# Two-block transformer forward pass on one core: the first block's attention loads the query latent's weights first, scores the second token half first, and turns keys after queries

## The reference, cut to what matters

```python
h = x @ w_in                                   # -> query latent c_q (256), k, v (2 heads x 64), k_idx (128), w_idx (8)
c_q = rms_norm(c_q, g_cq)
q, q_idx = c_q @ w_uq, c_q @ w_iq              # 16 heads x 64, 8 index heads x 128
k_idx = layer_norm(k_idx, g_ik, b_ik)
q, k, q_idx, k_idx = rope of each              # the first few columns of a head
# per block of 128 queries:
score = sum over index heads of w_idx * relu(q_idx . k_idx), causal
sel = the 64 keys of highest score             # per query
p = softmax of q . k over the selected keys; o = p . v
out = o @ w_o
```

## Time and profile before

| what | value |
|---|---|
| median of the three runs shown | 1112.74 us (1112.64 to 1114.21) |
| the profiled execution's own time | 1112.98 us |
| its span, first to last instruction | 1111.2 us |
| PE busy (matmuls) | 1081.2 us, 97% of the span |
| ACT busy | 547.6 us, 49% |
| DVE busy | 402.7 us, 36% |
| POOL busy | 775.8 us, 70% |
| chain of waits | PE 90%, DVE 7%, ACT 1%, DMA 1% |
| DMA | 186.45 MB, mean 168 GB/s |

### The profile page before, as it was taken

The page is one execution under the profiler, slowest core; times in us unless marked ns, Lnnn a source line. Parts: engine busy times, 40 slices in busy tenths (PEclk is TensorE's granted clock), DMA queues, the critical chain, the costliest instruction groups (busy, mean ns, idle before and its releaser), DMA issues.

```text
span 1111.2 us, 15697 instructions
## 1 busy us (share of the span) xinstructions
PE 1081.2 (97%) x6654; PEld 946.2 (85%) x6654; DVE 402.7 (36%) x741; ACT 547.6 (49%) x713; POOL 775.8 (70%) x201
## 2 busy tenths in 40 slices
PE   8978999999999997999999999999999999999997
PEld 7867888888889996888888899999999988888885
DVE  4674411119644787511110152821274233111103
ACT  6583453443357764544444256465565346343520
POOL 4723698788588741888878768686674768988880
PEclk9999999999999998999999999999999999999999
DMA  9211665555455431675555356454442555555541
GB/s 367 82 39 39 235 224 185 189 189 190 153 207 176 147 115 40 214 258 190 190 189 179 124 180 221 168 190 142 161 152 76 190 179 219 188 183 178 177 147 38
DMA packets 27445, 186.45 MB, mean 168 GB/s; under 512 B 3168, under 2 KB 3424, under 8 KB 5872
## 3 DMA queue, kind: packets, MB, share of 16 engines
q1 hardware_dynamic: 25184, 178.83, 46.4%
q10 hardware_dynamic: 2192, 6.62, 1.8%
HBM read 184.39 MB, written 1.05 MB: 167 GB/s over the span
## 4 chain that ended last, share of the span: by engine, by line
PE 90%; DVE 7%; ACT 1%; DMA 1%; issue 1%; DVEq 0%; SPq 0%; ACTq 0%
PE ps L380 27%; PE ps L382 27%; PE ps L381 27%; PE ps L1223 1%; DVE arena L2223 1%; PE ps L1370 1%; PE ps L2063 1%; PE ps L1088 1%; DMA stage<-in_tiles 1%; DVE arena L828 1%; DVE arena L850 1%; PE ps L2061 0%; PE ps L713 0%; DVE small L835 0%; DVE arena L1014 0%
## 5 line engine op out<-in xcount | busy, mean ns | idle before, releaser
L364 POOL TENSOR_TENSOR wl<-stage,wh 128x2048 fp32r<-128x2048 f32 x166 | 763.5, 4622 | 297.1 <-ACT wh L360 265.9
L360 ACT ACTIVATE wh<-stage 128x2048 fp32r<-128x2048 f32 (+1 forms) x168 | 319.9, 1906 | 114.4 <-DMA stage<-in_tiles 113.8
L380 PE MATMUL ps<-wh,xh 128*128 128x512 f32 (+2 forms) x832 | 306.1, 368 | 3.0 <-DVE xl L1642 1.6
L382 PE MATMUL ps<-wh,xl 128*128 128x512 f32 (+2 forms) x832 | 302.1, 363 | 0.0
L381 PE MATMUL ps<-wl,xh 128*128 128x512 f32 (+2 forms) x832 | 301.7, 363 | 0.0
L380 PEld LDWEIGHTS ps<-wh,xh 128*128 128x128 f32 x832 | 157.1, 189 | 27.3 <-DVE xl L1642 1.8
L382 PEld LDWEIGHTS ps<-wh,xl 128*128 128x128 f32 x832 | 157.0, 189 | 24.7
L381 PEld LDWEIGHTS ps<-wl,xh 128*128 128x128 f32 x832 | 157.2, 189 | 23.3
L380 PE MATMUL ps<-xh,wh 128*128 128x256 f32 x464 | 133.1, 287 | 0.0
L382 PE MATMUL ps<-xh,wl 128*128 128x256 f32 x464 | 131.3, 283 | 0.0
L381 PE MATMUL ps<-xl,wh 128*128 128x256 f32 x464 | 131.3, 283 | 0.0
(11 more groups left out here) (365 smaller groups left out, 1174.7 us busy)
## 6 DMA issues: line engine op xcount, KB each, us to landing
stage<-in_tiles SPq DMA_DIRECT2D x167, 1024.0 KB, 4.9
arena<-in_ln_g ACTq DMA_DIRECT2D x4, 512.0 KB, 3.6
arena<-in_ln_b ACTq DMA_DIRECT2D x4, 512.0 KB, 5.2
arena<-in_x_t SPq DMA_DIRECT2D x1, 1024.0 KB, 5.2
x_res<-in_x SPq DMA_DIRECT2D x1, 1024.0 KB, 20.4
out<-x_res SPq DMA_DIRECT2D x4, 256.0 KB, 2.1
stage<-in_tiles SPq DMA_DIRECT2D x1, 544.0 KB, 7.3
arena<-in_pre_mix_norm ACTq DMA_DIRECT2D x1, 512.0 KB, 7.7
```

Source lines behind the costliest of these rows:

```text
L360: nc.scalar.activation(wh[:, ring(n), part], stage[:, ring(n), part], ACT.Copy).then_inc(hi_done, 1)
L364: nc.gpsimd.tensor_tensor(wl[:, ring(n), :], stage[:, ring(n), :], wh[:, ring(n), :].bitcast(F32), ALU.subtract).then_inc(lo_done, 1)
L380: mm(out_, lh, rh, start=start, stop=False, skip_group_check=skip)
L382: return mm(out_, ll, rh, start=False, stop=stop, skip_group_check=skip)
```

## The change

Tile 0 is now the query latent's, loaded whole right behind `x_t`, and tile 1 the index keys' (1088 columns). ACT makes tile 0's high part in four quarters and only then issues the loads of positions and constants; DVE makes the low parts in quarters, and PE multiplies quarter by quarter. The latent has its own banks (0 and 3). Half 1's index queries, scores and selection come before half 0's; the index keys' rope stands behind the first index queries' rope on DVE; all of tile 3's products come late; the mask is made before the rope of half 1's queries. ACT's high parts have other places (tiles 8, 9 and 10 now stand together before the first exponentials), and warm-ups are moved. A line of "..." leaves out lines.

```diff
+    columns(w_att, 0, 256)
     tiles.append(np.concatenate([keys, np.zeros((P, TW - KD * IW), keys.dtype)], axis=1))
-    columns(w_att, 0, 256)
...
+            if n == 1:
+                sp.dma_start(stage[:, 1, 0:KD * IW], A["tiles"][1, :, 0:KD * IW]).then_inc(stage_in[1], 16)
...
-        his = [0]
+        his = [1]
...
-            first_low(dve, 0)
+            for c in range(4):
+                if c < 3:
+                    dve.wait_ge(first_hi.sem, c + 1)
+                else:
+                    dve.wait_ge(hi_done, 1)
+                first_low(0, slice(c * QUARTER, (c + 1) * QUARTER))
+            dve.wait_ge(hi_done, 2)
+            first_low(1, slice(0, KD * IW))
             dve.wait_ge(pos_in, 16)
             dve.wait_ge(c_in, 16)
...
-            first_low(dve, 1)
...
-            setup_loads(act)
             act.wait_ge(xt_in, 16)
             for c in range(4):
                 nc.scalar.activation(two(xh, c), two(x_raw, c), ACT.Copy).then_inc(xh_done.sem, xh_done.up())
+            act.wait_ge(stage_in[0], 16)
+            for c in range(4):
+                part = slice(c * QUARTER, (c + 1) * QUARTER)
+                ins = nc.scalar.activation(wh[:, 0, part], stage[:, 0, part], ACT.Copy)
+                if c < 3:
+                    ins.then_inc(first_hi.sem, first_hi.up())
+                else:
+                    ins.then_inc(hi_done, 1)
+            setup_loads(act)
...
-            keep_warm(7, 14)
+            keep_warm(7, 12)
+            for c in range(4):
+                pe.wait_ge(first_lo.sem, c + 1)
+                pe.wait_ge(x_ready.sem, x_ready.due(pe))
+                for m in range(2):
+                    for k in range(2 * c, 2 * c + 2):
+                        o = k * 256 + m * P
+                        last = mm3(ps[:, CQ_BANK[m], 0:T], (wh[:, 0, o:o + P], wl[:, 0, o:o + P]),
+                                   (xh[:, k, :], xl[:, k, :]), k == 0, k == KD - 1)
+            last.then_inc(used, 1)
...
-            tile_a(pe, 1, 0)
...
-            keep_warm(7, 6)
...
+            def keys_part(t, ks):
+                x = slice(t * P, (t + 1) * P)
+                for k in ks:
+                    o = k * 256
+                    last = mm3(ps[:, 2, t * T:(t + 1) * T], (xh[:, k, x], xl[:, k, x]),
+                               (wh[:, 3, o:o + T], wl[:, 3, o:o + T]), k == 0, k == KD - 1)
+                return last
+
+            def weigh(t, bank, width):
+                pe.wait_ge(dw_ready.sem, dw_ready.due(pe))
+                for h in range(IH):
+                    if h % (2 if t else 4) == 0:
+                        pe.wait_ge(relu_done.sem, relu_done.due(pe))
+                    last = mm(ps[:, bank, 0:width], dw[:, t * IH + h, :], relus[t][:, h, :], start=h == 0, stop=h == IH - 1)
+                last.then_inc(score_ps.sem, score_ps.up())
...
             pe.wait_ge(cq_ready.sem, cq_ready.due(pe))
-            query(2, 0, (4, 5)).then_inc(iq_ps.sem, iq_ps.up())
             pe.wait_ge(sq_done.sem, sq_done.due(pe))
             for t in range(2):
...
-            query(2, 1, (6, 7)).then_inc(used, 1)
-            index_turn(0)
+            query(2, 1, (6, 7)).then_inc(iq_ps.sem, iq_ps.up())
+            query(2, 0, (4, 5)).then_inc(used, 1)
+            index_turn(1)
+            pe.wait_ge(rs_cq.sem, 1)
...
+            late = (1, 3, 6, 7)
...
+            index_turn(0)
+            weigh(1, 0, T)
...
-            tile_b(pe, 3, [(1, 0, ps[:, 2, T:2 * T])])
+            low_ready(pe, 3)
+            keys_part(0, range(0, 4))
+            weigh(0, 1, P)
+            keys_part(0, range(4, KD))
+            keys_part(1, range(KD)).then_inc(used, 1)
+            pe.wait_ge(scored.sem, 2)
             query(4, 0, (1, 3)).then_inc(q_ps.sem, q_ps.up())
             query(4, 1, (6, 7)).then_inc(used, 1)
...
-            keep_warm(5, 4)
-            pe.wait_ge(q1_done.sem, q1_done.due(pe))
-            pe.wait_ge(scored.sem, 2)
-            for h in range(KD):
-                for t in range(2):
-                    last = nc.tensor.transpose(ps[:, 4 + h // 2, h % 2 * T + t * P:h % 2 * T + (t + 1) * P],
+            for t in range(2):
+                if t:
+                    pe.wait_ge(q1_done.sem, q1_done.due(pe))
...
-                if h % 2:
-                    last.then_inc(qt_ps.sem, qt_ps.up())
-            keep_warm(1, 8)
-            pe.wait_ge(kpad_done.sem, kpad_done.due(pe))
-            pe.wait_ge(qt_done.sem, qt_done.due(pe, 4))
-            pe.wait_ge(sel_done.sem, 1)
+                    if t and h % 2:
+                        last.then_inc(qt_ps.sem, qt_ps.up())
...
+                if i == 0:
+                    pe.wait_ge(kpad_done.sem, kpad_done.due(pe))
+                    pe.wait_ge(sel_done.sem, 1)
+                if i < 3:
+                    pe.wait_ge(qt_done.sem, (1, 2, 4)[i])
...
-            attend_pe(pe, HEADS // 2, logits, weighted)
+            attend_pe(pe, HEADS // 2, logits, weighted, 11)
...
+            act.wait_ge(used, 1)
+            act.wait_ge(c_in, 16)
+            for k in range(2):
+                last = nc.scalar.activation(hh[:, 20 + k, :], ps[:, CQ_BANK[k], 0:T], ACT.Copy, scale=gt[:, 44 + k:45 + k])
+            last.then_inc(cqh_done.sem, cqh_done.up())
...
+            hi_until(act, 3)
+            late_loads(act)
+            act.wait_ge(cq_ready.sem, cq_ready.due(act))
...
+            setup_act2(act)
...
-            hi_until(act, 3)
-            act.wait_ge(used, 2)
-            act.wait_ge(c_in, 16)
...
-            hi_until(act, 4)
...
+            hi_until(act, 4)
...
-            index_plain(0)
             index_plain(1)
+            index_turned(1)
+            for c, b in enumerate((1, 3, 6, 7)):
...
+                if c == 0:
+                    index_plain(0)
             index_turned(0)
             hi_until(act, 5)
-            index_turned(1)
-            hi_until(act, 6)
...
-            hi_until(act, 7)
+            hi_until(act, 6)
             act.wait_ge(used, 4)
...
-            hi_until(act, 8)
+            act.wait_ge(q_ps.sem, q_ps.due(act))
...
+            hi_until(act, 7)
+            act.wait_ge(kd_ps.sem, kd_ps.due(act))
...
-            act.wait_ge(kd_ps.sem, kd_ps.due(act))
...
             hi_until(act, 10)
...
+            dve.wait_ge(cqh_done.sem, cqh_done.due(dve))
+            for k in range(2):
...
+            last.then_inc(cq_ready.sem, cq_ready.up())
             ki = bank2(1)[:, :, 0:ID]
-            dve.wait_ge(used, 1)
+            dve.wait_ge(used, 2)
...
             dve.wait_ge(rs_cq.sem, rs_cq.due(dve))
+            index_rope(1)
+            keys_rope()
+            dve.wait_ge(kt_ps.sem, kt_ps.due(dve))
+            V.tensor_copy(kit, ps[:, 3, P:3 * P]).then_inc(kt_ready.sem, kt_ready.up())
+            dve.wait_ge(used, 3)
             index_rope(0)
...
+            V.tensor_copy(score[:, P:2 * P], ps[:, 0, 0:P])
+            V.tensor_tensor(score[:, 2 * P:3 * P], ps[:, 0, P:T], causal, ALU.min).then_inc(scored.sem, scored.up())
             dve.wait_ge(scored.sem, 1)
-            for i in range(4):
+            for i in range(5):
+                best_eight((1,))
+            dve.wait_ge(score_ps.sem, score_ps.due(dve))
+            V.tensor_tensor(score[:, 0:P], ps[:, 1, 0:P], causal, ALU.min).then_inc(scored.sem, scored.up())
+            dve.wait_ge(scored.sem, 2)
+            for i in range(TOPK // 8 - 5):
+                best_eight((1, 0))
+            for i in range(5):
                 best_eight((0,))
-            dve.wait_ge(score_ps.sem, score_ps.due(dve))
-            V.tensor_copy(score[:, P:2 * P], ps[:, 4, 0:P])
-            V.tensor_tensor(score[:, 2 * P:3 * P], ps[:, 4, P:T], causal, ALU.min).then_inc(scored.sem, scored.up())
-            dve.wait_ge(scored.sem, 2)
-            for i in range(TOPK // 8 - 4):
-                best_eight((0, 1))
-            for i in range(4):
-                best_eight((1,))
-            dve.wait_ge(used, 5)
...
             hi_until(act, 2)
-            late_loads(act)
-            setup_act2(act)
             dsa_act(act)
...
-            for n in range(2, 8):
+            for n in range(2, 7):
                 lo(pool, n)
             dsa_pool(pool)
+            lo(pool, 7)
```

More of the change, by code:

```diff
@@ L384, in low_ready @@
         def low_ready(pe, n):
-            if n < 2:
-                pe.wait_ge(first_lo.sem, n + 1)
+            if n == 1:
+                pe.wait_ge(first_lo.sem, 5)
             else:
@@ L694, in dsa_pe @@
             last.then_inc(kt_ps.sem, kt_ps.up())
-            tile_b(pe, 3, [(0, 0, ps[:, 2, 0:T])], done=False)
-            index_turn(1)
             pe.wait_ge(kt_ready.sem, kt_ready.due(pe))
+            late = (1, 3, 6, 7)
+            for h in range(IH):
+                if h % 4 == 0:
+                    pe.wait_ge(iqt_done.sem, iqt_done.due(pe))
+                last = mm(ps[:, late[h // 2], h % 2 * T:(h % 2 + 1) * T], iqt[:, h, P:T], kit, start=True, stop=True)
+                if h % 2:
```

(49 more changed lines are left out.)

88 lines of the change are left out of this document (36 added, 52 removed).

## The result

| | before | after |
|---|---|---|
| median of 12 runs | 1113.22 us | 1117.32 us |
| lowest and highest | 1112.64, 1120.80 | 1114.90, 1118.53 |
| profiled execution, its span | 1112.98, 1111.2 us | 1117.47, 1115.7 us |
| mean granted clock | 0.996 | 0.991 |
| first division | 68.57 | 72.53 |

The ratio is 1.0029 (95% interval 1.0020 to 1.0038), slower by more than the 0.2% that can be told from no change; the medians lie 4.10 us apart, and the new one is 1.5 us above the top of the range. Two executions of those behind this document, one of the kernel before at 1350.09 us and one of e5_forecast at 1201.0, ran at a mean granted clock of 0.75 and 0.85 and stand in no ratio. "First division" is DVE's RECIPROCAL of the first pair of heads, the point at which the forecast ended.

What follows compares the result with a forecast made beforehand. PE, busy 97% of the span, was taken as the bound, passing front changes on one for one. Logits 2.4 us earlier, then a third rounding, gave 67.1 - 66.6 = +0.45 us: 1113.2 us against the median, range 1110.8 to 1115.8.

Steps and rivals of the forecast that it cites:

- The term of 0.7 us for the landing after the last packet: Load of positions and constants: estimated 0.7 us from the last packet moved to the landing.
- the whole of 10.1 us: Load of positions and constants: 10.1 us from issue at 8.7 to landing at 18.8.
- Case (b): Late constants, issued not before the fourth quarter rounding: +1.4 us, 1114.6; chance 0.13.
- case (e): ACT's table switches cost twice 1.28 us, as if ACT had to run empty first: +2.6, 1115.8; chance 0.03.
- 1.4 us before DVE comes to them, so it hides: Index queries: PE is through at 27.5, ahead of DVE's rope at 28.9, so they add no time.
- case (c): PE's clock falls after idling before the index queries, matmuls near 0.6 us: +1.8, middle 1115.7; chance 0.13.
- ACT's three roundings: Tiles 8, 9, 10 before the first exponentials: 3 x 1.82 = 5.5 us, to 67.1, first division at 69.05.
- tile 7's is moved behind it: POOL before the loop: tile 6 ends near 50.4, 1.2 us before the keys' rope needs POOL; tile 7's work follows that rope.
- the 71 that the prediction had named as its limit: First division of the attention loop: the forecast is wrong if it comes before 67 or after 71.
- (d): The third rounding doesn't hold the exponentials, earlier logits passed on, no DVE wait before first division: -2.4, 1110.6; chance 0.09.
- from here the loop is as before: Attention loop from the first division on: no change, leaving the sum at +0.45 us.

Runs made afterwards that it cites:

- e5_forecast: Changed kernel with POOL's tile 8 low part behind the loop and ten warm-ups before PE's wait for the latent: 1114.01 us, ratio 0.9988.
- e4_rounds: Changed kernel with tiles 7 and 8 rounded in ACT's idle time behind tile 6, leaving two roundings before the exponentials: 1115.17 us, ratio 1.0017.
- e12_forecast_warm: e5_forecast with nine warm-ups behind the third logits in the loop: 1113.25 us, ratio 0.9994.
- e1_pool: Changed kernel with POOL's low part of tile 8 moved behind the loop's last division: 1115.25 us, ratio 1.0009.
- e8_port_before: Kernel before, with POOL starting tile 8's low part only when the first logits are in PSUM: 1116.69 us, ratio 1.0024.
- e3_consts: Changed kernel with positions and constants issued first in ACT's program, as before the change: 1111.98 us, ratio 0.9984.
- e7_behind: e6_all with tiles 9 and 10 also rounded behind the attention loop: 1108.00 us, ratio 0.9929.
- e11: Changed kernel with fifteen warm-ups behind the third logits: 1115.94 us, ratio 1.0015.
- e6_all: Changed kernel with the edits of e1_pool, e3_consts and e4_rounds together: 1108.17 us, ratio 0.9943.
- e10_control: Kernel before, with tiles 9 and 10 rounded behind the attention loop and POOL's tile 8 low part behind the divisions: 1113.79 us, ratio 0.9995.
- e2_warm: Changed kernel with ten warm-ups ahead of PE's wait for the latent's low part: 1115.58 us, ratio 1.0016.
- e9_loopwarm: Changed kernel with thirty warm-ups behind the third logits: 1117.87 us, ratio 1.0034.

## Why the prediction was wrong

**Right: the start.** The constants were issued at 8.74, beside the first quarter rounding, and took 9.60 us: 18.34 against 18.8. The term of 0.7 us for the landing after the last packet is in no row by itself; only the whole of 10.1 us has its measure, 9.60. The index keys ended at 21.37 (21.2), the squares at 23.87 (23.8). Case (b), an issue behind the fourth quarter, is out. ACT's two table loads took 1.28 us each and ACT was through at 27.3 (27.2), so case (e) is out, and with it the drain that the Trainium skill, ScalarE: Activation LUTs, "What ACT_TABLE_LOAD costs", adds to a switch: the trace does not agree, the sine starts at 25.18, 0.02 us behind the load, and the logarithm at 26.77, 0.01 us behind the second. DVE's first angle instruction took 0.94 us instead of 0.16, ending with POOL's tile 2 at 19.38; the constants' earlier landing hid it.

**Wrong, first step: "1.4 us before DVE comes to them, so it hides".** That sum ran the index queries at the full clock behind an idle of 2.6 us. The clock fell, the matmuls came every 0.43 us instead of 0.23 and lasted 0.63 us, which was case (c)'s own sign, and DVE's rope started at 31.28 instead of 28.9. Case (c) had the mechanism and the place, at +1.8 us; measured +2.4. Its chance of 0.13 was too small: rows 14 showed matmuls at both levels, and the warm-ups that stood against the idle were being removed. It also leaned on a wrong reading, that the longest idle of the kernel before after its start is 1.6 us. The trace has two longer ones. One is in the attention loop, and behind it the clock stayed at 1.00 (PE of the kernel before):

```profile
69.83 0.87 PE L788 MATMUL ps<-ident,arena 128*128 128x128 f32 x6 [2.90 <-DVE arena L850]
```

The other is the 4.76 us before 422.21. Behind it the clock read 0.50 from 422 to 426, and the page of the kernel before shows the fall in the 16th of its 40 slices:

```profile
PEclk9999999999999998999999999999999999999999
```

So this kernel already showed that an idle can cost the clock, and one as long as the forecast's that did not. From there everything to the first logits (62.74 against 60.35) is this one shift.

**Wrong, second step: the walk from the logits to the first division took only ACT's three roundings as new.** Those took 5.53 us as said. But moving tile 8's rounding there, and "tile 7's is moved behind it", had a second half that I did not price: tile 8's low part now waits for that rounding, and by e4_rounds it would come late without this wait too, since it stands behind tile 7's. Either way it falls into the loop's start. I had called POOL's work ready in time for PE and not asked what it does to DVE. DVE's scaling took 4.07 us instead of 0.17, and the division came a further 1.3 us late, at 72.53, past the 71 that the prediction had named as its limit. Its sign for (d), no wait of DVE before the division, was there and misled: what had been a wait for ACT now lay inside the record of L877.

**Wrong, third step: "from here the loop is as before".** PE's idle before its transposes was 2.90 us before the change and 4.43 after, and the clock fell: 1.06 us. Even the forecast itself held a longer idle than before (3.13 us in e5_forecast), and there too the clock fell.

At the third division the four terms are 0.23 (e12_forecast_warm against before, forecast 0.45), 2.42 (31.28 against 28.86, the rope of e12_forecast_warm), 1.06 (loop) and, as what is left, 1.31 for POOL, which is also what e1_pool gave (1.86 less 0.55): together the 5.02 measured. The span shows 4.5 of it, for the reason near 430 us given above, which is chance and not the change's doing. The sum's sign, its first term and the landing were right; two of the three costs were outside any case, which is why even the top of (c), 1116.4, fell short.

**The port.** The runs show DVE's scaling and its cast held until POOL's subtraction ends, and the mask and the maxima not. The Trainium skill, SBUF — State Buffer, "Who interferes with whom", says this: cast and tensor_scalar can, for some operands, enter a mode that takes the pair of SBUF ports shared with GpSimd, under an exclusive lock, while tensor_reduce never does; the trace agrees (4.07 us against 0.42 and 0.68). That the lock is what holds them is the skill's account; the runs show who holds whom, and until when. Read against the new order of POOL's program, it gave a rival with up to 4.5 us, the length of POOL's instruction, as its price.

## What to carry to other kernels

When an order is changed, list for every engine what now runs beside the critical stretch, and not only what waits for what. A GpSimd elementwise instruction of 4.5 us on SBUF that slides under a chain of short VectorE instructions can hold one of them almost as long (4.07 us here) and put what hangs on it back, by 1.3 us in the changed kernel and 2.4 in e8_port_before; a warm-up taken out, or a wait lengthened, can cost the clock and so nearly double the matmuls behind it (0.43 us against 0.23). Small loads that the first half of a kernel hangs on go out ahead of everything, even where the queue's own work seems to leave room.

## What was not expected of the hardware

**Which VectorE instructions GpSimd held.** The held one ended with POOL's instruction every time:

| run | POOL's subtraction ends | held instruction ends | its length, unheld |
|---|---|---|---|
| after, CAST L525 | 19.36 | 19.38 | 0.94, 0.16 |
| after, L877 | 70.47 | 70.51 | 4.07, 0.17 |
| e3_consts, L877 | 64.91 | 64.94 | 4.07, 0.17 |
| e4_rounds, L877 | 68.59 | 68.62 | 2.92, 0.17 |
| e8_port_before, L838 | 69.10 | 69.12 | 2.54, 0.17 |

Not held beside a running POOL: the mask (one operand in PSUM, 0.96 us) and the maxima (0.42 and 0.68 us), as the rows of e8_port_before show. Nor, though both sides are in SBUF, the MAX8 and MATCH_REPLACE8 of the selection over 256 columns: 0.43 and 0.41 us at 44.49 and 45.03 of the changed kernel, beside POOL's tile 5, and the same at 52.73 and 53.27 of the kernel before, where POOL stood idle.

**The clock after an idle PE.** The length of the idle alone does not tell what the clock does. These are the idles ahead of the first transposes of the loop, and what the clock read behind them:

| runs | idle, us | granted clock behind it |
|---|---|---|
| e7_behind, e11, e12, e6_all | 0.53 to 1.33 | 1.00 |
| before, e10_control | 2.90 | 1.00 |
| e1_pool | 3.13 | 1.00 |
| e4_rounds | 3.27 | 1.00 |
| e5_forecast | 3.13 | 0.57 |
| after, e2_warm, e3_consts | 4.42 to 4.43 | 0.50 |
| e8_port_before | 5.28 | 0.50 |

In front of the index queries it fell in all five runs that had an idle of over 1 us there: 2.64 us in the changed kernel's profile and 2.98 to 3.12 in e1_pool, e4_rounds, e9_loopwarm and e11. What tells 3.13 us from 3.13 us, and 2.64 from 3.27, stays open. At the index queries the time of the fall differs as well: in these four runs the clock is already down in part between 22 and 24 us (0.57 to 0.71), with PE still idle, and back at 1.00 from 30 us on. In the changed kernel's profile it is 1.00 until 24 us and still 0.78 from 30 to 32. So the same index queries were through, by the rope's start, at 31.28 there and at 30.54 to 30.73 in those four, which left them alone. The changed kernel's times spread with the clock: its runs reach from 1114.9 us, at a mean granted clock of 0.994, to 1118.5, at 0.989, where 8 of the 12 runs of before lie within 0.8 us.
